# Spreading the inverse roots of the second norm over the partitions: through device memory instead of through TensorE

## What is computed

```python
x = x + jnp.einsum('bsm,md->bsd', mix, w_out[l])
h = rmsnorm(x, norm2_w[l])
x = x + conv_glu(h, ffn_w_up[l], ffn_conv_w[l], ffn_conv_b[l], ffn_w_down[l])

def rmsnorm(x, w):
    y = x * lax.rsqrt(jnp.mean(x * x, axis=-1, keepdims=True) + EPS)
    return y * w

def conv_glu(h, w_up, conv_w, conv_b, w_down):
    gate, val = jnp.split(jnp.einsum('bsd,df->bsf', h, w_up), 2, axis=-1)
    gate = causal_dwconv(gate, conv_w, conv_b)
    return jnp.einsum('bsf,fd->bsd', gelu(gate) * val, w_down)
```

## Time and profile before

| what | value |
|---|---|
| median of 3 runs | 414.7 us (414.54 to 414.77) |
| the profiled execution's own time | 414.7 us |
| its span, first to last instruction | 412.8 us |
| PE busy | 408.1 us, 99% of the span |
| DVE busy | 306.2 us, 74% |
| ACT busy | 259.8 us, 63% |
| mean granted TensorE clock | 1.000 |
| share of PE in the chain that ended last | 96% |

### The profile page before, as it was taken

One profiled execution on the slowest core, in us unless ns is written; L12 is line 12 of the kernel. 1 busy time (PEld: TensorE's weight loads), 2 busy tenths in 40 slices (PEclk: granted clock), 3 DMA queues, 4 the chain that ended last, 5 costly groups with the idle time before them and its releaser, 6 DMA issues.

```text
span 412.8 us, 6404 instructions
## 1 busy us (share of the span) xinstructions
PE 408.1 (99%) x2464; PEld 357.5 (87%) x2464; DVE 306.2 (74%) x435; ACT 259.8 (63%) x351; POOL 34.7 (8%) x26
## 2 busy tenths in 40 slices
PE   8999999999999999999999999999999999999996
PEld 8999999888888799888888888888888888888885
DVE  4988798746865879669867788777677766776775
ACT  5778877794489765897636565653555555545640
POOL 3132534411011000000000000000000000000000
PEclk9999999999999999999999999999999999999999
DMA  8845793475362522225552446645455564455202
GB/s 306 339 159 170 293 322 137 166 202 223 139 241 102 206 102 103 103 102 205 203 203 104 157 171 236 214 156 216 182 197 203 184 211 174 150 203 195 103 0 102
DMA packets 12637, 74.12 MB, mean 180 GB/s; under 512 B 1332, under 2 KB 2760, under 8 KB 4424
## 3 DMA queue, kind: packets, MB, share of 16 engines
q1 hardware_dynamic: 12616, 73.83, 49.9%
HBM read 72.75 MB, written 1.07 MB: 179 GB/s over the span
## 4 chain that ended last, share of the span: by engine, by line
PE 96%; DVE 1%; DMA 1%; ACT 0%; POOL 0%; issue 0%; DVEq 0%; POOLq 0%; ACTq 0%
PE pj L1783 17%; PE pj L1347 13%; PE pj L1349 13%; PE pj L1348 13%; PE pj L1784 10%; PE mx L1397 6%; PE mx L1348 6%; PE mx L1349 6%; PE mx L1347 6%; PE pj L1786 2%; PE mx L1394 2%; DMA x_pad<-in_x 1%; DVE wlo L818 1%; PE pj L1446 0%; PE pj L1450 0%; PE pj L1442 0%
## 5 line engine op out<-in xcount | busy, mean ns | idle before, releaser
L818 DVE TENSOR_TENSOR wlo<-w_b,whi 128x2048 fp32r<-128x2048 f32 x58 | 132.8, 2290 | 51.9 <-ACT whi L405 51.9
L405 ACT CAST whi<-w_b 128x2048 fp32r<-128x2048 f32 x63 | 120.1, 1908 | 35.3 <-PE pj L1349 29.7
L1783 PE MATMUL pj<-hT,whi 128*128 128x512 f32 x308 | 109.0, 395 | 0.0
L1784 PE MATMUL pj<-hT,wlo 128*128 128x256 f32 x352 | 95.1, 280 | 0.0
L1783 PEld LDWEIGHTS pj<-hT,whi 128*128 128x128 f32 x308 | 57.8, 188 | 13.5 <-issue 0.3
L1784 PEld LDWEIGHTS pj<-hT,wlo 128*128 128x128 f32 x352 | 66.4, 189 | 1.8
L1347 PE MATMUL pj<-hT,whi 128*128 128x256 f32 x208 | 59.4, 286 | 0.0
L1349 PE MATMUL pj<-hT,wlo 128*128 128x256 f32 x208 | 58.9, 283 | 0.0
L1348 PE MATMUL pj<-hT,whi 128*128 128x256 f32 x208 | 58.9, 283 | 0.0
L1347 PEld LDWEIGHTS pj<-hT,whi 128*128 128x128 f32 x208 | 39.7, 191 | 0.7 <-issue 0.7
L1348 PEld LDWEIGHTS pj<-hT,whi 128*128 128x128 f32 x208 | 39.7, 191 | 0.0
(11 more groups left out here) (248 smaller groups left out, 630.3 us busy)
## 6 DMA issues: line engine op xcount, KB each, us to landing
w_b<-in_w_in SPq DMA_DIRECT2D x23, 1024.0 KB, 4.9
w_b<-in_w_up SPq DMA_DIRECT2D x22, 1024.0 KB, 4.8
w_b<-in_w_down SPq DMA_DIRECT2D x11, 1024.0 KB, 4.8
w_b<-in_w_out SPq DMA_DIRECT2D x8, 1024.0 KB, 4.8
seg_b<-ld_rows SPq DMA_DIRECT2D x4, 512.0 KB, 6.6
x_pad<-in_x SPq DMA_DIRECT2D x2, 512.0 KB, 3.7
w_b<-in_w0c SPq DMA_DIRECT2D x1, 512.0 KB, 6.4
Wm_b<-m_rows_d SPq DMA_DIRECT2D x1, 512.0 KB, 5.6
```

Source lines behind the costliest of these rows:

```text
L405: nc.scalar.copy(whi[:, slot, :], wraw[:, slot, :]).then_inc(s.hi_done, 1)
L818: nc.vector.tensor_tensor(wlo[:, slot, :], wraw[:, slot, :], whi[:, slot, :].bitcast(F32), ALU.subtract).then_inc(s.lo_done, 1)
L1783: nc.tensor.matmul(ps, whi[:, slot, w], hT[:, k, :, :], start=k == 0, stop=False, skip_group_check=True)
L1784: ins = nc.tensor.matmul(ps[:, 0:T], wlo[:, slot, w], hT[:, k, 0, :], start=False, stop=False, skip_group_check=True)
```

## The change

The two diagonals, the products with ones, and the copy out of PSUM go, and with them PE's wait for the diagonals and its wait for rbc ahead of the first down unit. The reciprocal is called ahead of the low parts of the second half of x. ACT's queue stores the two columns of reciprocals as one row in device memory (two DMAs of 128 x 4 bytes), casts a unit, waits until both have landed, and loads the row with a broadcast source into rbc (128 partitions x 1 KB). DVE's first `gate_scale` waits for that load in place of the copy.

```diff
+        r2_row = nc.dram_tensor("r2_row", [1, T], F32)
...
+            act.wait_ge(s.r2_ready, 1)
+            for t in range(NT):
+                act.dma_start(r2_row.ap()[:, t * P:(t + 1) * P].rearrange("o p -> p o"), stat[:, 38 + t:39 + t]).then_inc(s.r2_kept, 16)
             split(step_unit(0, 0))
+            act.wait_ge(s.r2_kept, 16 * NT)
+            act.dma_start(rbc[:, :], r2_row.ap().to_broadcast([P, T])).then_inc(s.r2_spread, 16)
             low_copy(0, 0)
             split(step_unit(0, 1))
             ffn_steps(act, step)
...
                 nc.vector.reciprocal(stat[:, 38:40], stat[:, 36:38]).then_inc(s.r2_ready, 1)
-                dve.wait_ge(s.r2_ready, 1)
-                for t in range(NT):
-                    nc.vector.tensor_scalar(rdiag[:, t, :], ident[:, :], stat[:, 38 + t:39 + t], None, ALU.mult).then_inc(s.rdiag_ready, 1)
...
             x2_ms()
+            x2_root()
             x2_lo(1)
-            x2_root()
...
                 if b == 0:
-                    dve.wait_ge(s.rbc_ready, 1)
+                    dve.wait_ge(s.r2_spread, 16)
...
             split(step_unit(0, 0))
-            dve.wait_ge(s.rbc_ps, 1)
-            nc.vector.tensor_copy(rbc[:, :], bank[0][:, 0:T]).then_inc(s.rbc_ready, 1)
             halves_sum(0, 0)
...
-            def spread_r():
-
-                pe.wait_ge(s.rdiag_ready, NT)
-                for t in range(NT):
-                    ins = mm(bank[0][:, t * P:(t + 1) * P], ones[:, :], rdiag[:, t, :])
-                ins.then_inc(s.rbc_ps, 1)
-
...
             def down(i, b, slot, unit, first=False, last=False):
-                if first:
-                    pe.wait_ge(s.rbc_ready, 1)
                 pe.wait_ge(s.glo, i + 1)
...
             up(0, U_FFN % NR, rest, s.h2_lo).then_inc(s.unit_done, 1)
-            spread_r()
             up(1, (U_FFN + 1) % NR, rest).then_inc(s.unit_done, 1)
```

More of the change, by code:

```diff
@@ L179, in build @@
             yg_ready yg_sq yg_sum yg_ssq yg_ms yg_rt yg_r ssmT_hi ssmT_lo x2_att x2_g0
-            x2_ps x2_ready ssq2 ms2 rt2 r2_ready rdiag_ready rbc_ps rbc_ready h2_ps h2_hi h2_lo gscaled
+            x2_ps x2_ready ssq2 ms2 rt2 r2_ready r2_kept r2_spread h2_ps h2_hi h2_lo gscaled
             low_copied summed gbase gtap gconv gact gprod ghi glo tail_added last_ps res_ready out_done""".split()
```

## The result

| | before | changed |
|---|---|---|
| median | 414.69 us (5 runs) | 420.83 us (5 runs, 420.33 to 422.25) |
| ratio | | 1.0152, 95% interval 1.0142 to 1.0163 |
| span of the profiled execution | 412.8 us | 419.0 us |
| PE busy | 408.1 us | 409.3 us |
| mean granted TensorE clock | 1.000 | 0.996 |

Forecast were 414.24 us and a range of 413.9 to 415.1. The time came out on the side of the first rival, and far behind it.

A forecast was written before the change was run, and what follows sets the result against it. PE was taken to bound the kernel, busy 408.1 of 412.8 us. Removing the product with ones took 0.46 us off 414.7, all other terms costing or giving nothing: 414.24 us, range 413.9 to 415.1.

The forecast's parts named there:

- rival 1: The first rival, at ACT's wait: stores land late, at 5.6 us; low copy 2.3 us late, 416.1 us; chance 0.06.
- the product with ones: On PE at the end of the second up unit: removing its four passes takes 0.46 us off the time.
- The reciprocal moved ahead: On DVE ahead of the low parts: its 0.16 us fits into 1.00 us of idling, so it costs nothing.
- The slack of the chain to glo: In step 0, between glo set and the first down product: some 0.90 us, 0.44 with PE coming 0.46 earlier.
- ACT's wait for the stores: On ACT ahead of the low copy: stores land after 2.7 us, low copy on time with 0.6 us to spare.
- The prediction's own rule: At the low copy: its lateness, less 0.90 us of slack ahead of the first down product, is added to the time.
- the two issues: On ACT ahead of its cast: two stores' issues of 0.43 us each, occupying it until 230.80; cost nothing.
- The queueing behind the weight load: In the DMA engines: small writes wait for the load to drain, landing near 233.2; spare time 0.5 us.
- Rival 4: Two trips through device memory, each with a fixed cost: 7.1 us, ending at 237.5, inside 239.46; no chance of its own.

The follow-up runs named there:

- no_spread: The changed kernel without its three transfers and ACT's waits, rbc a constant 1; 414.21 us against 414.65 for the kernel before (ratio 0.9989).
- pairs: The changed kernel with one store of 128 x 8 bytes in place of two of 128 x 4; 415.44 us against 414.78 before (ratio 1.0018).
- late_wait: The changed kernel with ACT's wait and the spread's issue moved behind the first half's low copy and second half's cast; 425.67 us against 414.78.
- turned: The changed kernel with VectorE turning the columns first, so each store writes 4 runs of 128 bytes; 414.35 us against 414.78 before (ratio 0.9992).
- quads: The changed kernel with one store of 128 x 16 bytes in place of two of 128 x 4; 414.26 us against 414.59 before (ratio 0.9992).
- spaced64: The changed kernel with the 4-byte pieces stored 64 bytes apart and the spread reading another row; 414.25 us in one run.
- the first two probes: The kernel before plus seven extra stores of various shapes from ACT's queue, awaited only by idle GpSimd; one run each, the second 416.03 us.

## Why the prediction was wrong

- **Right:** PE bound this part, and the product with ones cost 0.46 us (no_spread: 0.44 between the medians, with 0.1 to 0.8 inside the interval). The reciprocal moved ahead cost nothing: it ran at 228.65, and the low parts came on time. The slack of the chain to glo held to 0.01 us: in pairs glo was 1.92 us late and PE 1.03 later than before, where 0.90 of slack gives 1.02.
- **Wrong by its size, in the step "ACT's wait for the stores":** "The write is of the first kind, so I take 2.7". It took 5.9 and, for the store that counted, 10.8. I had named the 4-byte pieces as a point for rival 1 and then priced that rival by the 5.6 us median of reads in long rows, and given it 0.06. No row showed a store of small pieces, so the upper end was a guess from another kind of transfer; all stores in the trace had pieces of at least 1 KB. "Every store seen took at most 2.7" rested on the four stores of x alone: for the two stores of rows at 40 us, the nearest in kind, the view gives no landing. Rival 1's mechanism was the true one. Its point of decision, a landing of 5.0 us behind an issue at 230.37, means 235.4 on the trace's clock; in pairs the store landed at 235.28 and the kernel lost 0.66 us, which fits.
- **Wrong in the path:** lateness was priced only through glo. PE stood first at its next up unit, for DVE's sum (L1255), with the low copy 6.31 us late and PE 5.06. The prediction's own rule with the measured landing, 6.31 - 0.90, gives 420.1 us; the missing 0.7 us is about what the lower clock added.
- **Left out:** the lower clock behind a stall of PE. It stretched PE's work by 1.6 us, of which some 0.9 counted in the end (estimate above). Behind the 0.87 us of waiting in pairs the granted clock stayed at 1.00.
- **Left out:** what slow stores do to transfers behind them. In the changed kernel it cost nothing extra, as its spread was issued behind the stores' landing; in late_wait the spread took 8.9 us.
- **Wrong without effect:** the two issues were to hold ACT for 0.86 us. They ran beside ACT's own activations, and the cast began at 229.95 as before. Where the issues took longer, in turned, the cast did wait for them (0.76 us idle, at 230.75).
- **The queueing behind the weight load** that I had weighed put the small writes' landing at 233.2. Where the pieces were not the trouble they landed at 233.3 (quads) and 233.8 (spaced64), 4.3 to 4.6 us after the issue, and their packets passed only between 232 and 233 us: waiting for the load is real, and it left only 0.4 to 0.8 us of the cover. The rule of the Trainium skill that the prediction names for it (DMA: Bandwidth & Descriptors, section "Queues, rings and completion order": a DMA engine changes queues only at whole packets) agrees with the trace.
- **Rival 4:** the fixed cost of about 2.0 us is given in the Trainium skill, DMA: Bandwidth & Descriptors, section "Anatomy of one DMA", for DMAs that GpSimd issues; these were issued by ACT. Nothing in the sum rested on it.

## What to carry to other kernels

A column of one 4-byte value per partition isn't a small transfer: stored side by side into device memory, 128 of them took 6 to 14 us here, and transfers issued behind them came late too. Put at least 16 bytes of each partition together, or turn the column into runs first, before such a store, and look for its landing and not its kilobytes. When a wait is priced, the upper end for an operation the trace doesn't show must come with the question what the wait does at that end: here every microsecond beyond 0.9 of slack went to the engine that bounds the kernel, and its clock made it dearer.

## What the runs showed that I had not expected

- Dense small writes: see the table of shapes. Spacing of 32 bytes or pieces of 16 bytes bring 128 pieces from 6 to 14 us down to 1.6 to 2.5, and to 4.5 beside the weight load of this place (quads).
- Such a store delays others: weight loads landed after 9.8 and 9.9 us in place of 4.9, a spread after 10.4. The load's bytes were late, and of the spread only the completion.
- A DMA issued from ACT's queue runs beside the ACT instructions ahead of it: the issues at 228.85 and 229.24 lie beside the high parts from 228.88 on, and the cast kept its place. An instruction behind the issues starts after them, as the cast in turned shows.
- A store of four runs of 128 bytes from partitions 32 apart took 1.06 us to issue (turned, at 229.06; 1.03 and 1.06 in the first two probes), against 0.35 for one of 128 pieces. The second of two in a row took 0.49, against 0.45.
- After PE had stood for 4.9 us it was granted half its clock for some 3 us, which stretched its work by 1.6 us; after 0.87 us of standing it kept the full clock.
